# The norm vector of the feed-forward parts: from the first weights to the transposed activations

## The reference

```python
def _rmsnorm(x, g):
    xf = x.astype(jnp.float32)
    y = xf * lax.rsqrt(jnp.mean(xf * xf, axis=-1, keepdims=True) + EPS)
    return (y * g.astype(jnp.float32)).astype(x.dtype)

def _sqrelu_mlp(h, w1, w2):
    return jnp.square(jax.nn.relu(h @ w1)) @ w2

x = x + _sqrelu_mlp(_rmsnorm(x, mlp_norm[i]), mlp_w1[i], mlp_w2[i])
```

## Time and profile before

| | |
|---|---|
| median of 3 runs | 1649.92 us (1649.57 to 1650.88) |
| profiled execution | 1646.14 us |
| its span | 1644.4 us |
| mean granted clock of TensorE | 0.997 |
| PE busy | 1598.6 us, 97% of the span |
| PEld busy | 1329.6 us, 81% |
| DVE busy | 816.6 us, 50% |
| ACT busy | 599.7 us, 36% |
| POOL busy | 355.9 us, 22% |
| HBM read | 132.33 MB |

### The profile page before, as it was taken

The page is one execution under the profiler, slowest core; times in us unless marked ns, Lnnn a source line. Parts: engine busy times, 40 slices in busy tenths (PEclk is TensorE's granted clock), DMA queues, the critical chain, the costliest instruction groups (busy, mean ns, idle before and its releaser), DMA issues.

```text
span 1644.4 us, 23363 instructions
## 1 busy us (share of the span) xinstructions
PE 1598.6 (97%) x8858; PEld 1329.6 (81%) x8866; DVE 816.6 (50%) x1468; ACT 599.7 (36%) x1068; POOL 355.9 (22%) x534
## 2 busy tenths in 40 slices
PE   7999988999999999999999999999989999999999
PEld 6776655888888888899988889998767888888887
DVE  4456566444444444444647576546564443434342
ACT  5433333432323233434434443434442432323230
POOL 3412100050000000263528364535621000000000
PEclk9999999999999999999999999999999999999999
DMA  6211110223232323332222412222223232323232
GB/s 170 83 59 40 54 38 14 90 90 107 85 112 80 115 77 104 127 90 78 65 77 77 129 54 78 65 78 65 86 71 116 77 106 86 110 82 103 88 101 79
DMA packets 77562, 139.93 MB, mean 85 GB/s; under 512 B 12192, under 2 KB 12192, under 8 KB 77216
## 3 DMA queue, kind: packets, MB, share of 16 engines
q1 hardware_dynamic: 75280, 134.51, 26.9%
q10 hardware_dynamic: 2192, 4.20, 0.7%
HBM read 132.33 MB, written 6.36 MB: 84 GB/s over the span
## 4 chain that ended last, share of the span: by engine, by line
PE 84%; DVE 5%; POOL 4%; issue 2%; ACT 2%; SPq 1%; DMA 0%; ACTq 0%; POOLq 0%; DVEq 0%
PE ps L467 74%; PE ps L525 3%; PE ps L555 2%; POOL qrs L1332 2%; PE ps L567 2%; PE ps L539 2%; DVE pT_sb L1112 1%; POOL qss L1331 1%; PE ps L498 1%; ACT w_h L786 1%; DVE qss L1023 1%; ACT sq L824 1%; ACT p_sb L850 1%; PE ps L519 1%; DVE ps L1056 0%
## 5 line engine op out<-in xcount | busy, mean ns | idle before, releaser
L467 PE MATMUL ps<-w_h,act_h 128*128 128x512 f32 x768 | 317.1, 413 | 5.4 <-DVE w_l L997 3.4
L467 PE MATMUL ps<-w_h,act_l 128*128 128x512 f32 x768 | 307.0, 400 | 0.0
L467 PE MATMUL ps<-w_l,act_h 128*128 128x512 f32 x768 | 305.8, 398 | 0.0
L786 ACT ACTIVATE w_h<-w_raw,gain_t 128x512 fp32r<-128x512 f32 x316 | 209.8, 717 | 148.3 <-PE ps L467 102.4
L997 DVE SCALAR_TENSOR_TENSOR w_l<-w_raw,gain_t,w_h 128x512 fp32r<-128x512 f32 x316 | 226.8, 759 | 59.1 <-ACT w_h L786 59.0
L467 PE MATMUL ps<-w_h,hid_h 128*128 128x512 f32 x640 | 252.7, 395 | 0.1
L467 PE MATMUL ps<-w_l,hid_h 128*128 128x512 f32 x640 | 250.1, 391 | 0.0
L467 PE MATMUL ps<-w_h,hid_l 128*128 128x512 f32 x640 | 249.5, 390 | 0.0
L467 PEld LDWEIGHTS ps<-w_h,act_h 128*128 128x128 f32 x768 | 192.0, 250 | 24.3 <-issue 7.9
L467 PEld LDWEIGHTS ps<-w_l,act_h 128*128 128x128 f32 x768 | 192.1, 250 | 16.0
L467 PEld LDWEIGHTS ps<-w_h,act_l 128*128 128x128 f32 x768 | 193.0, 251 | 14.4
(11 more groups left out here) (150 smaller groups left out, 1847.5 us busy)
## 6 DMA issues: line engine op xcount, KB each, us to landing
w_raw<-in_mlp_w SPq DMA_DIRECT2D x128, 512.0 KB, 3.7
w_raw<-in_dil_w_in SPq DMA_DIRECT2D x72, 512.0 KB, 3.7
w_raw<-in_fox_w_in SPq DMA_DIRECT2D x22, 512.0 KB, 3.6
w_raw<-in_fox_w_out SPq DMA_DIRECT2D x8, 512.0 KB, 3.8
w_raw<-in_dil_w_out SPq DMA_DIRECT2D x8, 512.0 KB, 3.8
acc_kept<-acc SPq DMA_DIRECT2D x2, 1056.0 KB, 6.6
o_sb<-acc_kept SPq DMA_DIRECT2D x2, 1056.0 KB, 5.2
x_sb<-in_x SPq DMA_DIRECT2D x4, 512.0 KB, 8.5
```

Of the source, the lines that this page charges most:

```text
L467: return mm(ps_out, lhs[i], rhs[j], start=(k == 0 and term == 0), stop=(k == KT - 1 and term == 2))
L786: last = fn(w_h[:, u % WR, j, :], raw(u)[:, j, :], ACT.Copy, scale=gain_t[:, norm, k:k + 1])
```

## The change

The multiplication by the norm vector moves. `unit_gain` returns no vector for the units of the feed-forward parts any more, so their first weights are split as they are, by the single instructions for both pieces. In `prepare`, for the preparations 2 and 5 alone, DVE first multiplies the transposed block in PSUM by the vector, as a broadcast operand, into the scratch tile `sq`; ACT copies the high part from `sq`, and DVE subtracts from `sq` too. A new semaphore, `scaled`, tells ACT that the scratch tile is full. As there is only one such tile, DVE waits until its own subtraction of the block before is done (`actl_done`) before it multiplies again.

```diff
-            for layer in range(2):
-                if BANK_MLP[layer] <= u < BANK_MLP[layer] + 16 * CHUNKS:
-                    return 2 * layer + 1 if (u - BANK_MLP[layer]) % 16 < 8 else None
             return None
...
             def prepare(n, half, t):
 
                 act.wait_ge(prep_full, prep_no(n, t, half) + 1)
-                nc.scalar.copy(prep_dst(n, half, t)[0],
-                               prep_bank(n, t, half)[:, :].rearrange("p (k t) -> p k t", k=4)).then_inc(acth_done, 1)
+                src = prep_bank(n, t, half)
+                if n in PREP_OF_MLP:
+                    act.wait_ge(scaled, scale_no(n, t, half) + 1)
+                    src = sq
+                nc.scalar.copy(prep_dst(n, half, t)[0], src[:, :].rearrange("p (k t) -> p k t", k=4)).then_inc(acth_done, 1)
...
             def prepare(n, half, t):
 
                 high, low = prep_dst(n, half, t)
+                src = prep_bank(n, t, half)[:, :].rearrange("p (k t) -> p k t", k=4)
+                if n in PREP_OF_MLP:
+                    dve.wait_ge(prep_full, prep_no(n, t, half) + 1)
+                    dve.wait_ge(actl_done, prep_no(n, t, half))
+                    tmp = sq[:, :].rearrange("p (k t) -> p k t", k=4)
+                    gain = gain_t[:, PREP_OF_NORM.index(n), 4 * half:4 * half + 4].unsqueeze(2).broadcast_to([P, 4, P])
+                    v.tensor_tensor(tmp, src, gain, ALU.mult).then_inc(scaled, 1)
+                    src = tmp
                 dve.wait_ge(acth_done, prep_no(n, t, half) + 1)
-                v.tensor_tensor(low, prep_bank(n, t, half)[:, :].rearrange("p (k t) -> p k t", k=4), f(high),
-                                ALU.subtract).then_inc(actl_done, 1)
+                v.tensor_tensor(low, src, f(high), ALU.subtract).then_inc(actl_done, 1)
```

More of the change, by code:

```diff
@@ L289, in trunk @@
             sem("s_full"), sem("max_done"), sem("exp_done"), sem("pt_full"), sem("pt_done"), sem("pv_done"), sem("o_done"))
-        earg_done, efac_done, merged, normed = sem("earg_done"), sem("efac_done"), sem("merged"), sem("normed")
+        scaled, earg_done, efac_done, merged, normed = sem("scaled"), sem("earg_done"), sem("efac_done"), sem("merged"), sem("normed")
         acc_out, acc_in, x_out = sem("acc_out"), sem("acc_in"), sem("x_out")
@@ L305, in trunk, with scale_no @@
         PREP_OUT = [1, 4]
+        PREP_OF_MLP = [2, 5]
+        def scale_no(n, t, half):
+            return 8 * PREP_OF_MLP.index(n) + 4 * half + t
         X_ADDS = [0, 8, 8 + 8 * CHUNKS, 16 + 8 * CHUNKS]
```

## The result

The changed kernel took 1652.36 us (median of 13 runs, 1650.81 to 1656.99), the kernel before 1649.52 (13 runs, 1645.73 to 1652.67). The ratio is 1.0026 with a 95% interval of 1.0015 to 1.0036, so 2.5 to 5.9 us slower. The medians are 2.84 us apart.

A forecast was written before the change was run, and what follows sets the result against it. TensorE, busy 97% of the span, was taken as the bound: removed work 0, a longer wait for the last transposed block 1.2 us per layer, +2.4 on 1649.92, giving 1652.3 us; range 1650.2 to 1654.6.

The forecast's parts named there:

- the sum: Whole kernel: 1.2 us added per layer at the feed-forward start, +2.4 us in all, nothing coming back later.
- Removed work is worth nothing: First-weight splits: about 18 us of ACT and 12.8 us of DVE work saved beside unbroken matmuls, costed at 0 us.
- rival 3: Feed-forward matmuls: TensorE gets faster when ACT and DVE work less, returning 1.6 us, to 1650.7 us; chance 6%.
- The price of each step: Instruction durations: split 1.05 on ACT and 1.22 on DVE, multiplication 0.69, copy 0.61, subtraction 0.69 us.
- The high end of the range: Feed-forward starts: DVE and ACT steps 10% over their rows, last addition 0.3 late; 1.9 us per layer, 3.8 in all.
- The chain to the last block: Feed-forward start: last addition to x through multiplications, copies and subtractions to the matmul, 4.97 us, making it 1.15 us later.
- The replay of the bank before: Output projection: two blocks in one bank delay the next addition 0.8 us, eaten up by the last; 0.05 allowed.
- rival 4: Output projection: a longer pile in the queue makes the additions slip, 0.5 us more per layer, 1653.3 us; chance 7%.
- rival 1: Feed-forward starts: TensorE's clock drops behind the longer wait, 1.4 us lost each, 1653.7 or 1655.1 us; chance 15%.
- The signs named ahead: Trace: 144 splits, 16 multiplications, waits 1.2 to 1.6 us, pace 0.2269, last addition unmoved; wrong if clock under 1.00 behind waits.
- The bounds of no change: Whole kernel: about 0.2%, 3.3 us, counts as the same, 1646.6 to 1653.2 us; same was given 70%.
- the case to which 25% had been given: Whole kernel: slower beyond the no-change bounds, from 7 of the forecast, 15 of the clock rival and 3 more; 25%.

The follow-up runs named there:

- the changed kernel again: The changed kernel, no edit, profiled a second time against the kernel before: 1649.59 us, ratio 1.0016 (1.0005 to 1.0026); also called the second comparison.
- the removed part alone: Changed kernel with transposed blocks made as before, so the feed-forward norm vector is left out; ratio to the kernel before 1.0002 (0.9993 to 1.0012).
- The added part alone: Changed kernel with first weights still split with the vector, so it is multiplied in twice; 1654.17 us, ratio to the kernel before 1.0039.

## Why the prediction was right, and where its terms were off

The forecast was 1652.3 us, measured were 1652.36. That they agree so closely is partly luck: the sum was +2.4, its true size without a clock drop is +3.3 (the stretches of the changed kernel again), and the median of before had come down from 1649.92 to 1649.52.

- *Removed work is worth nothing.* Right: 0 +- 0.02 us in the stretches of the removed part alone. The rule that counts VectorE operations (rival 3) would have had a gain, and none of it came, though DVE did have 2.0 us less to do.
- *The price of each step.* Right for all durations, within 0.01 us. (The high end of the range counts five DVE and ACT steps; its own list has six. With six it comes to 1.85, so the 1.9 stands.)
- *The chain to the last block.* Right in its order; mis-sized in its gaps. The forecast took 0.03 us for DVE to ACT and for DVE waiting on itself. The rows have 0.09 (328.02 + 0.68 to 328.79) and 0.11 (329.44 + 0.69 to 330.24). Twice 0.06 and once 0.08 are the 0.2 by which the chain grew beyond 4.97.
- *The replay of the bank before.* Right that two blocks in one bank push the next addition back and that the last one would hardly be late; the same gaps, added over two rounds, made it 0.26 instead of 0.05. That slipping is rival 4's mechanism, at less than half its price (0.21 more than allowed for, against 0.5). The added part alone showed the other half of the step: without the lighter splits it is a microsecond more per layer, as the prediction said.
- *The sum.* What was mis-sized is the cost per layer, by the gaps above: 1.2 us forecast, 1.6 measured, inside the 1.9 of the high end. Nothing came back later, as said: 313.10 us behind the wait in both kernels.
- *The clock (rival 1).* It happened in 2 of the 8 waits of 1.4 to 2.4 us in the four profiles with them, behind 1.81 and 2.39 us; each time at 1.6 us, where 1.4 was worked out. In the ten starts of a feed-forward part with a wait of 0.2 us or none, it never did. Two of these four profiles had a drop, one of the two of the changed kernel, so 15% looks too low, but four are few. What decides whether a wait is followed by a drop stays open.
- *The signs named ahead.* The groups of 144, the 16 multiplications and the pace of 0.2269 came as said. Three did not: the wait was to be 1.2 to 1.6 us and was 1.81, the last addition was to be where it was and came 0.26 late, and a granted clock under 1.00 behind a wait, named as a sign of being wrong, was seen in the second layer.
- *The bounds of no change.* 1.0026 is slower than by 0.2%, the case to which 25% had been given, but its interval (1.0015 to 1.0036) reaches to both sides of 0.2%; 1.0016 in the second comparison is under it. A step of 3.3 us sits on that edge.

## What to carry to other kernels

Work taken off engines that run beside a saturated TensorE was worth nothing here, except for the two splits that stand in the queues ahead of the last addition; and a step added ahead of the one block that TensorE waits for was paid in full; look for that block first, it is the one made last before a stage. Count the gaps between the engines as well as the durations: the six hand-overs of this chain had 0.6 us of them. Where such a chain cannot be shortened, give TensorE matmuls that do not need the block: the first half of a second bank, 2.7 us of work that has to be done anyway, covered the wait of 1.8 at no cost. And where whole executions scatter by more than the effect, compare one stretch of the trace between two fixed matmuls.

## What the runs showed of the hardware that was not expected

- A VectorE instruction of 512 columns that waits for the VectorE instruction just before it starts 0.80 us after that one's start; without the wait, in the kernel with two scratch tiles, 0.61. The Trainium skill says that in a chain of eight VectorE copies a semaphore after each costs nothing extra over one after the last ("VectorE: DVE Perf Modes", section "The DRAIN you can't avoid"). Here the wait on the instruction just before costs 0.19 us, at all four such places of the profile of the changed kernel.
- Half clock came behind waits of 1.81 and 2.39 us, each in a stream of dense matmuls at full clock, and stayed away behind others of 1.81, 1.89 and 2.39 us. The length of the wait alone does not decide it.
- TensorE's pace of 0.2269 us per matmul of 512 columns did not move when ACT and DVE beside it had some 31 us less to do together (the removed part alone: ACT 599.7 to 580.2 us, DVE 816.6 to 804.7).
